# SiLU gates as x/2 · (1 + tanh(x/2)): ScalarE takes the tanh out of PSUM, VectorE multiplies

## The reference, cut to what matters

```
h = rms_norm(x, g_in[layer])
proj = h @ w_in[layer]
qA, kA, vA, qB, kB, vB, qM, gate, qI, kI, wI = jnp.split(proj, split_points, axis=-1)
...
oA = dilated_mixture_attention(qA, kA, vA, slopes_a)     # 8 heads
oB = dsa_attention(qB, kB, vB, qI, kI, wI, slopes_b)     # 4 heads, the 256 best keys of each token
oM = memory_attention(qM, kM, vM)                        # 4 heads, 256 memory tokens
o = jnp.concatenate([oA.reshape(B, T, W_A), oB.reshape(B, T, W_B), oM.reshape(B, T, W_M)], axis=-1)
o = o * jax.nn.silu(gate)
x = x + o @ w_out[layer]
return rms_norm(x, g_final)
```

## Time and profile before

| | |
|---|---|
| median of 3 runs | 773.7 us (770.96 to 774.82) |
| the profiled execution | 768.31 us, its span 766.5 us |
| mean granted TensorE clock | 0.982 |
| busy in the span: PE, DVE, ACT, POOL | 697.1, 435.5, 334.3, 131.7 us |

### The profile page before, as it was taken

How to read it: one execution, slowest core, us unless ns; L and a number is a source line. 1 busy time by engine, 2 the same in 40 slices (tenths; PEclk the granted TensorE clock), 3 DMA queues, 4 the chain that set the end, 5 groups by cost and what they waited for, 6 DMA issues and landing times. The chain is left out here.

```text
span 766.5 us, 11469 instructions
## 1 busy us (share of the span) xinstructions
PE 697.1 (91%) x4229; PEld 546.3 (71%) x4229; DVE 435.5 (57%) x1012; ACT 334.3 (44%) x633; POOL 131.7 (17%) x94
## 2 busy tenths in 40 slices
PE   2889999898999999899989998999979967899996
PEld 2668888666777777677767776777767655678884
DVE  4765775267464586647664786479733445322433
ACT  4466665344353344424442444345635446321411
POOL 1111111001210221131113111411140024011320
PEclk9999999999999999999999999999999996999999
DMA  8311113011111321211121112111110117204331
GB/s 307 93 55 28 28 28 82 2 27 42 42 28 42 97 56 42 73 49 32 42 75 45 33 42 75 47 33 42 28 69 6 38 45 239 77 15 160 104 117 56
DMA packets 53175, 48.76 MB, mean 64 GB/s; under 512 B 5744, under 2 KB 45696, under 8 KB 53120
## 3 DMA queue, kind: packets, MB, share of 16 engines
q1 hardware_dynamic: 53120, 48.02, 20.6%
HBM read 40.15 MB, written 7.86 MB: 63 GB/s over the span
## 5 line engine op out<-in xcount | busy, mean ns | idle before, releaser
L1250 PE MATMUL j_ps<-h_hi,w_hl 128*128 128x512 f32 (+1 forms) x624 | 208.8, 398 | 0.9 <-issue 0.9
L1250 PEld LDWEIGHTS j_ps<-h_hi,w_hl 128*128 128x128 f32 (+1 forms) x624 | 115.7, 185 | 26.0 <-issue 1.5
L572 POOL TENSOR_TENSOR w_hl<-w_raw,w_hl 128x1024 fp32r<-128x1024 f32 (+1 forms) x30 | 70.8, 2360 | 360.8 <-ACT w_hl L665 360.8
L1250 PE MATMUL j_ps<-h_lo,w_hl 128*128 128x512 f32 (+1 forms) x312 | 121.7, 390 | 0.0
L817 ACT ACTIVATE prob<-prob,nmax 128x256 f32<-128x256 f32 (+7 forms) x128 | 89.7, 702 | 51.2 <-DVE nmax L1094 42.8
L805 ACT ACTIVATE probT<-pt_ps 128x512 f32<-128x512 f32 (+3 forms) x88 | 41.4, 470 | 131.7 <-PE pt_ps L1361 131.0
L1250 PE MATMUL s_ps<-h_hi,w_hl 128*128 128x512 f32 x240 | 79.0, 398 | 0.4 <-POOL w_hl L572 0.4
L1361 PE MATMUL pt_ps<-ident,prob 128*128 128x128 f32 x496 | 75.1, 286 | 4.5 <-DVE gate L1121 3.8
L1361 PEld LDWEIGHTS pt_ps<-ident,prob 128*128 128x128 f32 x496 | 54.1, 143 | 25.2 <-issue 21.2
L1020 DVE TENSOR_SCALAR_CACHE_REDUCE picked<-idx,tk 128x384 f32<-128x384 f32 (+5 forms) x72 | 67.8, 942 | 1.4
L1250 PEld LDWEIGHTS j_ps<-h_lo,w_hl 128*128 128x128 f32 (+1 forms) x312 | 58.1, 186 | 11.0
(11 more groups left out here) (213 smaller groups left out, 1058.9 us busy)
## 6 DMA issues: line engine op xcount, KB each, us to landing
w_raw<-in_w_in_dram SPq DMA_DIRECT2D x28, 512.0 KB, 3.8
bias<-in_a_tab_dram SPq DMA_DIRECT2D x8, 512.0 KB, 4.7
mixed_scratch<-gate SPq DMA_DIRECT2D x14, 256.0 KB, 2.4
bias<-mixed_scratch SPq DMA_DIRECT2D x8, 448.0 KB, 5.1
bias<-in_w_out_dram SPq DMA_DIRECT2D x6, 512.0 KB, 3.8
idx<-in_x_dram SPq DMA_DIRECT2D x4, 512.0 KB, 5.2
probT<-in_w_mem_kv_dram SPq DMA_DIRECT2D x4, 512.0 KB, 6.6
prob<-in_x_dram SPq DMA_DIRECT2D x4, 512.0 KB, 4.4
```

The costliest lines, as they stand in the source:

```text
L572: pool.tensor_tensor(w_hl[:, w % 2, 1, :, 0:n], w_raw[:, :, 0:n], w_hl[:, w % 2, 0, :, 0:n].bitcast(F32), ALU.subtract).then_inc(w_lo_read ...
L1250: last = pe.matmul(bank[0:n, :], a[:, k, 0:n], c[:, k, HALF * b:HALF * b + HALF], start=(k == 0 and q == 0), stop=(k == KD - 1 and q == 2))
```

## The change

ACT's copy of a gate half out of PSUM becomes a tanh with scale 0.5, and the SiLU over the whole tile, its wait and its semaphore are dropped. The gate projections join those that have a part on DVE: `split_low` gets a branch that writes (tanh + 1) times the bank, which holds x. The factor 1/2 goes into the inverse sums: the copy that spreads them becomes a multiplication by 0.5. `finish_group` waits for the DVE part of the gate's second half. Because `is_split` now names gates, the bank of a gate half is free only after the DVE part.

```
@@ is_split
-            return what in ("kIwI", "qI", "k", "kvB") or (what == "q" and PAIRS[p][0] != "M")
+            return what in ("kIwI", "qI", "k", "kvB", "gate") or (what == "q" and PAIRS[p][0] != "M")
@@ evacuate (ACT)
-                        last = act.activation(gates(p)[:, cut], bank[:, :], ACT.Copy)
+                        last = act.activation(gates(p)[:, cut], bank[:, :], ACT.Tanh, scale=0.5)
...
-                if kind == "w" and W_TILES[w][0] == "gate" and b == 1:
-                    act.wait_ge(j_free, m + 1)
-                    act.activation(gates(W_TILES[w][1]), gates(W_TILES[w][1]), ACT.Silu).then_inc(gate_ready, 1)
@@ split_low (DVE)
+                elif what == "gate":
+                    last = dve.scalar_tensor_tensor(out=gates(p)[:, cut], in0=gates(p)[:, cut], scalar=1.0,
+                                                    in1=bank[:, :], op0=ALU.add, op1=ALU.mult)
@@ invert_sums (DVE)
-                dve.tensor_copy(linv[:, :, :, :], inverse.unsqueeze(3).broadcast_to([P, 4, 2, DH])).then_inc(linv_ready, 1)
+                dve.tensor_scalar(linv[:, :, :, :], inverse.unsqueeze(3).broadcast_to([P, 4, 2, DH]), 0.5, None,
+                                  ALU.mult).then_inc(linv_ready, 1)
@@ finish_group (DVE)
-                dve.wait_ge(gate_ready, sum(w <= W_OF["gate", p] for (what, _), w in W_OF.items() if what == "gate"))
+                dve.wait_ge(j_split, splits(use_number["w", W_OF["gate", p], 1] + 1))
```

More of the change, by code:

```diff
@@ L315, in build_program @@
         v_kept = sem("v_kept")
-        gate_ready = sem("gate_ready")
         idx_scored = sem("idx_scored")
```

## The result

| | before | changed |
|---|---|---|
| first measurement, median us | 773.7 (770.96 to 776.19, 5 runs) | 781.07 (775.57 to 781.5, 5 runs) |
| again, both beside each other (experiment 6) | 772.76 (29 runs) | 779.02 (6 runs) |
| profiled execution: span us, mean granted clock | 766.5, 0.982 | 773.8, 0.976 |

The ratio is 1.0087, 95% interval 1.0051 to 1.0124; the second time 1.0081 (1.0052 to 1.0111). Slower, by about 6.5 us. The forecast was 778.0, with a range that ends at 781.0: the first median lies at that end (781.07; the ratio times 773.7 is 780.4).

The account below looks back on a forecast made before the run. PE, busy for 697.1 of 766.5 us, sets the time. ACT's 0, pair 0's 1.6 and pair 5's 2.7 add 4.3 to 768.3, giving 772.6; with 5.4 from profiled execution to median, 778.0, range 771.5 to 781.0.

Parts of the forecast that it names:

- ACT, -29 us, worth 0: All eight gates: ACT loses 8 SiLUs and 16 table loads, 29 us of 334; gain on PE's path 0.
- 447: DVE's busy time, forecast near 447 us, from 435.5 and 11 us for 16 products at 0.69.
- A tanh evacuation costs what the copy did; inverse sums at nothing: Gate evacuations on ACT stay at 0.60 us; the 16 multiplications spreading inverse sums on DVE cost nothing.
- Collision in pair 0, +1.6: Pair 0: POOL's L572 starts sooner, holds DVE's L1021, and PE's transposes wait 1.6 us longer.
- Pair 5, +2.7: Pair 5: two products 1.4, with a held L1021 +2.35 at PE's transposes; 0.35 more at the last gate; together 2.7.
- The sum, +4.3: Whole kernel: 0 from ACT, 1.6 in pair 0, 2.7 in pair 5; 768.3 becomes 772.6 us.
- the 5.4 us between its execution and the median: Added to 772.6 us because the runs' median lies 5.4 above the profiled execution, giving 778.0.
- 1 (no collisions): Pairs 0 and 5: collisions don't come, pair 0 costs 0, pair 5 1.4; median 775.1 us; chance 0.25.
- 5 (all covered): Whole kernel: everything is covered, pair 5 too; 773.7 us; chance 0.03.
- 2 (faster, ACT paces): Steps after a gate: ACT paces them, PE's uncovered stops go, 4.7 us; median 769.0; chance 0.12.
- 3 (the bank at 16 halves): All 16 gate halves: PE's next work waits for the product, 0.69 each, 11 us; median 784.7; chance 0.08.
- 4: ACT: tanh lies in another table set than exp, so the loads stay; 775 us; chance 0.02.

Follow-up runs that it names:

- experiment 6: The changed kernel, unedited, run and profiled again beside the kernel before: ratio 1.0081, 779.02 us against 772.76.
- run 1: The kernel before with ACT's SiLU and so its table loads taken out, no product on DVE, the gate's nonlinearity left out: ratio 1.0048.
- run 2: The changed kernel with a SiLU of a constant table into a spare tile at the old places, so all table loads are back: ratio 1.0050.
- run 3: The changed kernel, but in step 4 of each pair POOL starts its long operation only after DVE's first product (L1121): ratio 1.0072.
- run 8: The changed kernel with POOL waiting as in run 3, and both gate products of pair 5 moved to later or other places on DVE: ratio 1.0047.
- run 9: Run 8 with the spare SiLU of a constant table put back on ACT at all gates: ratio 1.0012.
- run 10: The changed kernel with the spare SiLU of a constant table at pair 0's gate alone: ratio 1.0016.
- run 4: The changed kernel with 20 useless PE transposes in pair 0's long wait, plus a PE wait for the gate to leave the bank: ratio 1.0036.
- run 12: Run 8 with 17 useless PE transposes in pair 0's two waits, and run 4's added wait ahead of the scores of step 4: ratio 1.0003.
- run 11: The changed kernel with the spare SiLU of a constant table at the seven other gates, none at pair 0: ratio 1.0064.
- run 7: The kernel before with run 3's edit, POOL waiting before its long operation: ratio 0.9989.

## Why the prediction was right, and where it was not

- **ACT, -29 us, worth 0.** Measured -28.7, and worth less than nothing: run 1. (DVE came to 453.6 and not to 447: the held operations count as busy, and I had not added them.)
- **A tanh evacuation costs what the copy did; inverse sums at nothing.** Right, 594 and 474 ns.
- **Collision in pair 0, +1.6.** Right: held 1.68 us, 1.5 us on the path; absent in runs 2, 3, 8, 9 and 10. The Trainium skill's rule ("SBUF — State Buffer", two separate sides), that a VectorE operation with two SBUF inputs and a GpSimd operation exclude each other, agrees: 1.68 and, in pair 5, 2.06 us for an operation of 0.16, each ending with POOL's.
- **Pair 5, +2.7.** Measured 2.9, differently composed: the two products cost 1.85 rather than 1.4, the collision behind them (2.06 us at 527.76) 0.24 rather than 0.95 (a fill on PE hid most of it), and the last gate's products 0.8 rather than 0.35. That the sum fits is luck: two errors of 0.45 upward and one of 0.7 downward. Run 8 takes the first two back.
- **The sum, +4.3.** As work it holds: the traces give 4.3, run 6's rest 3.5 +- 0.4. **The step that failed is that this was the whole sum**: "0 + 1.6 + 2.7" has no term for the granted clock. The stop of 3.02 us brought a second piece of 1.7 lost, which cost PE 0.3 to 1.0 us in the traces, and the runs show 2.1 +- 0.9 us more lost in all; 3.5 + 2.1 = 5.6 in means, and 6.3 by the medians of the second pair, 6.7 by the first ratio, against the 4.3 forecast. Where the rest of the 2.1 arises is open. I could have asked: the profile before showed a clock of 0.982, and I added the 5.4 us between its execution and the median as a constant. Between 4 and 5 us of that is clock (13.8 lost against 18.6).
- **The chances.** I gave 0.48 to no difference beyond 0.5% and 0.42 to slower by more. Slower by more came, with the lower end of the interval at 1.0051.
- **Rivals.** 1 (no collisions) and 5 (all covered): refuted by the held L1020s. 2 (faster, ACT paces): refuted by run 1, and pair 6's wait is still 1.34 us at 595.95. 3 (the bank at 16 halves): a bank wait in pair 5 only. 4: three loads, it does what it says.

The clock's part in words: PE stops longer, and the chip answers with the lower of its two clocks, 1.2 GHz, behind the stop, when the critical work has resumed. The Trainium skill ("TensorE: Matmul & The Clock Gate", Part 1) says that a monitor in the hardware watches PE's activity, halves the clock of an idle array and gives it back to a busy one, and that its watch runs on freely, not in step with the program. Runs 4 and 12, where useless work on PE takes one piece away at pair 0 each, agree with the first; that the same kernel has a fall in one profile and not in the next (before, 14.5 and 19.6 lost) fits the second, which no run tests.

**Open.** Runs 3 and 8 have no collision, and each shows one piece at pair 0 like before; still their runs lose 1.8 and 3.7 us more. One profile each can't tell where. Without SiLU PE's two stops ahead of the values and of the transposes of pair 0 are shared out otherwise (0.79 and 1.50 us where they were 1.52 and 0.77, the same sum), which may raise the chance of a fall, but that was not isolated. Nor was run 11's +1.1 against run 6's +2.1 settled; their errors overlap.

## What to carry to other kernels

When you free an engine off the path, ask what its next work will start sooner, and what of another engine's that lands on: here 29 us less of ACT moved a GpSimd operation 2.5 us forward, onto a chain of tiny DVE operations that PE waited for. Read the granted clock of several executions before you take a profile as the baseline, and give a PE stop that grows a price of its own beyond its length: here, from 1.50 to 3.02 us, one more piece at half clock, 0.3 to 1.0 us on the path. A product that takes PSUM must go where DVE is idle: in the one pair without slack the two products cost 0.59 and 1.26 us, and moving each by one place took both back. And look at what an added wait costs before you judge a filler: in runs 4 and 12 it took 0.9 to 1.0 us.

## What the runs showed of the hardware that was not expected

- TensorE's clock falls in pieces of 1.7 us lost, sometimes two or three together. Before had 14.5 us of it in one profile and 19.6 in the other, and its 29 runs of one session spread over 9.5 us (768.62 to 778.16); the clock explains most of that (correlation -0.93; in the other two sessions -0.83 and -0.90). A piece lost costs less than 1.7 us where PE waits meanwhile.
- Useless transposes in PE's waits can give time back: run 12 against run 8, 1.0003 against 1.0047, though the wait that they needed cost 0.9 us.
- A collision can cost nothing: that of pair 5 in the kernel before did (run 7 takes it away and gains nothing). In the changed kernel a 128x1 operation is held for almost all of POOL's:
```profile
549.93 2.38 POOL L571 TENSOR_TENSOR w_hl<-w_raw,w_hl 128x1024 fp32r<-128x1024 f32 x1 [20.12 <-ACT w_hl L664]
549.93 2.39 DVE L1035 SCALAR_TENSOR_TENSOR tk<-tk 128x1 f32<-128x1 f32 x1
```
It makes PE 1.42 us late at 552.81 and PE has it back by 559.27, where a wait of 1.84 us is now 0.45.
